# Four RMS norms of a two-block transformer kernel: sums by tokens in two columns, spread into rows by TensorE, and one weight load placed between two halves

## The reference, cut to what matters

```python
def rmsnorm(x, g):
    y = x * lax.rsqrt(jnp.mean(x * x, axis=-1, keepdims=True) + 1e-6)
    return y * g

# first block
for l in range(2):
    h = h + hybrid_mixer(rmsnorm(h, norm_mix[l]), ...)          # norm1 of layer l
    h = h + expert_choice_ffn(rmsnorm(h, norm_ffn[l]), ...)
x = rmsnorm(h, norm_final)                                      # f norm
# second block
x = x + sincos_2d(256)
sh1, sc1, gt1, sh2, sc2, gt2 = split(silu(c) @ ada_w + ada_b, 6)
hx = rms_norm(x, norm1_g) * (1 + sc1) + sh1                     # x norm
x = x + gt1 * token_mixer(hx @ w_in, ...)
x = x + gt2 * hier_moe(rms_norm(x, norm2_g) * (1 + sc2) + sh2, ...)
return rms_norm(x, final_norm_g)                                # l norm
```

## Time and profile before

| what | value |
|---|---|
| median of 3 runs | 2142.53 us (2142.21 to 2148.26) |
| profiled execution, whole | 2147.99 us |
| its span from first to last instruction | 2146.2 us |
| PE busy | 1917.2 us (89%) |
| DVE busy, ACT busy | 645.6 us (30%), 545.4 us (25%) |
| DMA | 748.52 MB, mean 349 GB/s |

### The profile page before, as it was taken

One profiled execution on the slowest core, in us unless ns is written; L12 is line 12 of the kernel. 1 busy time (PEld: TensorE's weight loads), 2 busy tenths in 40 slices (PEclk: granted clock), 3 DMA queues, 4 the chain that ended last, 5 costly groups with the idle time before them and its releaser, 6 DMA issues.

```text
span 2146.2 us, 32065 instructions
## 1 busy us (share of the span) xinstructions
PE 1917.2 (89%) x14254; PEld 1185.0 (55%) x14254; DVE 645.6 (30%) x992; ACT 545.4 (25%) x837; POOL 0.2 (0%) x4
## 2 busy tenths in 40 slices
PE   9999998787878999999898988889999998878796
PEld 8988832121312898872333433359999644444443
DVE  4476500000000548641431111057657300000001
ACT  4366300000000347530201222033544211011111
POOL 0000000000000000000000000000000000000000
PEclk9999999999999999999999999999999999999999
DMA  9734999999999962699999999974426999999996
GB/s 355 263 129 167 397 418 428 428 428 428 428 428 415 369 228 80 239 377 421 426 423 419 421 424 421 428 271 157 157 80 233 416 425 428 429 423 427 424 426 267
DMA packets 123028, 748.52 MB, mean 349 GB/s; under 512 B 6288, under 2 KB 27152, under 8 KB 83344
## 3 DMA queue, kind: packets, MB, share of 16 engines
q1 hardware_dynamic: 122896, 746.52, 85.3%
HBM read 745.45 MB, written 1.05 MB: 348 GB/s over the span
## 4 chain that ended last, share of the span: by engine, by line
PE 55%; DMA 37%; DVE 4%; ACT 2%; issue 1%; SPq 0%; DVEq 0%; ACTq 0%
PE bank L802 19%; DMA ring<-w_expert_up 12%; PE bank L893 10%; DMA ring<-w_expert_down 10%; PE bank L946 8%; DMA ring<-w_expert_gate 5%; PE bank L805 5%; DMA ring<-moe_w_up 5%; DMA ring<-moe_w_down 3%; DMA arena<-moe_w_up 2%; PE bank L924 2%; PE bank L829 1%; PE bank L1097 1%; PE bank L1118 1%; PE bank L1170 1%
## 5 line engine op out<-in xcount | busy, mean ns | idle before, releaser
L893 PE MATMUL bank<-ring,arena 128*32 128x512 f32 (+1 forms) x3232 | 518.2, 509 | 85.1 <-DMA ring<-w_expert_up 39.4
L893 PEld LDWEIGHTS bank<-ring,arena 128*32 128x32 f32 x3232 | 164.8, 109 | 407.4 <-issue 210.9
L946 PE MATMUL bank<-ring,arena 128*32 128x512 f32 x1280 | 279.3, 606 | 48.2 <-DMA ring<-w_expert_down 38.5
L802 PE MATMUL bank<-arena_parts,ring_parts 128*128 128x256 f32 x1296 | 293.9, 283 | 0.0
L802 PEld LDWEIGHTS bank<-arena_parts,ring_parts 128*128 128x128 f32 x1296 | 218.6, 189 | 6.6 <-ACT arena_parts L1722 2.3
L946 PEld LDWEIGHTS bank<-ring,arena 128*32 128x32 f32 x1280 | 68.8, 111 | 238.9 <-issue 171.0
L1722 ACT ACTIVATE arena<-bank 128x512 f32<-128x512 f32 (+1 forms) x142 | 73.7, 544 | 452.3 <-PE bank L908 216.3
L2265 DVE TENSOR_TENSOR arena<-arena,bank 128x512 f32<-128x512 f32 x24 | 15.8, 685 | 553.7 <-PE bank L893 553.7
L802 PE MATMUL bank<-extra_parts,ring_parts 128*128 128x256 f32 x512 | 144.2, 282 | 0.0
L802 PE MATMUL bank<-ring_parts 128*128 128x256 f32 x688 | 132.4, 284 | 1.8 <-DVE ring_parts L2694 0.9
L802 PEld LDWEIGHTS bank<-ring_parts 128*128 128x128 f32 x688 | 109.0, 189 | 4.0 <-DVE ring_parts L2694 1.2
(11 more groups left out here) (385 smaller groups left out, 2391.1 us busy)
## 6 DMA issues: line engine op xcount, KB each, us to landing
ring<-w_expert_down SPq DMA_DIRECT2D x62, 2048.0 KB, 24.0
ring<-w_expert_gate SPq DMA_DIRECT2D x58, 2048.0 KB, 23.4
ring<-w_expert_up SPq DMA_DIRECT2D x54, 2048.0 KB, 25.6
ring<-w_in SPq DMA_DIRECT2D x32, 2048.0 KB, 11.7
ring<-moe_w_up SPq DMA_DIRECT2D x24, 2048.0 KB, 28.3
ring<-moe_w_gate SPq DMA_DIRECT2D x20, 2048.0 KB, 37.9
arena<-moe_w_down SPq DMA_DIRECT2D x16, 2048.0 KB, 34.0
ring<-ada_w SPq DMA_DIRECT2D x12, 2048.0 KB, 16.9
```

The lines of the kernel that those rows point to most:

```text
L802: last = pe.matmul(out[:, n * S:(n + 1) * S], w[:, k, n * P:(n + 1) * P], x[:, k, :], start=first, stop=final)
L893: last = pe.matmul(to[own_rows(half, e)].rearrange("p (q c) -> p q c", c=own), x_slots[:, c, 32 * e:32 * e + 32], w[:, k, half], start=c = ...
L946: last = pe.matmul(banks[4 + e // PAIRS][own_rows(half, e), :].rearrange("p (x d) -> p x d", x=2), hidT[:, e // PAIRS * own + f % own, own ...
```

## The change

For norm1 of layer 1, f norm, x norm and l norm the squared chunk becomes the weight side of the sum: 16 products of one column each (8 chunks, two halves of 128 tokens), which leave the sums of 256 tokens as two columns of 128 partitions. Root and reciprocal work on 128x2. DVE then multiplies the identity by the two columns into two diagonal blocks, and PE multiplies a tile of ones by them, which puts the row of inverse roots on every partition of the PSUM bank; the eight products read that bank in place of SBUF. The 16 idle products behind x norm's sums become 8 behind f norm's rows and 6 behind x norm's rows. In layer 1 the load of unit 18 goes between unit 0's two halves. The 20 idle products of layer 0 are written at another place in the loop, with nothing between the old place and the new one, since `ADA_WITH[0]` has no entry for unit 0.

```diff
+        root_cols, inv_cols = rms[:, 0:TH], rms[:, TH:2 * TH]
+        inv_diag = rms_inv.rearrange("p (h t) -> p h t", h=TH)
...
+            def token_sums_part(step, sq, j, out, prior, **back):
+                pe.wait_ge(act_done, act_at(f"{prior} {j}", loops, **back))
+                for k in (2 * j, 2 * j + 1):
+                    for half in range(TH):
+                        last = pe.matmul(out[:, half:half + 1], sq[:, k, half * P:(half + 1) * P], ones[:, 0:1],
+                                         start=k == 0 and half == 0, stop=k == DC - 1, skip_group_check=True)
+                if j == 3:
+                    last.then_inc(pe_done, pe_p.mark(step + " sum"))
+
+            def inverse_rows(step, out, **back):
+                pe.wait_ge(dve_done, dve_at(step + " diag", loops, **back))
+                pe.matmul(out[:, 0:S], ones, rms_inv, start=True, stop=True).then_inc(pe_done, pe_p.mark(step + " rows"))
...
                 for j in range(4):
-                    sum_squares_part("norm1", squares, j, norm_bank, "squares")
+                    if layer:
+                        token_sums_part("norm1", squares, j, norm_bank, "squares")
+                    else:
+                        sum_squares_part("norm1", squares, j, norm_bank, "squares")
+                if layer:
+                    inverse_rows("norm1", take(6, "dve", "hn1 3"))
...
             for j in range(4):
-                sum_squares_part("f norm", hn3, j, norm_bank, "f squares")
+                token_sums_part("f norm", hn3, j, norm_bank, "f squares")
+            inverse_rows("f norm", take(6, "dve", "first block 3"))
+            idle_products(banks[4], 8)
             norm_bank = take(7, "act", "x norm root")
             for j in range(4):
-                sum_squares_part("x norm", hn3, j, norm_bank, "x squares")
-            idle_products(banks[4], 16)
+                token_sums_part("x norm", hn3, j, norm_bank, "x squares")
+            inverse_rows("x norm", take(7, "dve", "x normed 3"))
+            idle_products(banks[4], 6)
...
-            root("f norm", bank=banks[6])
+            root("f norm", TH, root_cols, banks[6])
...
+            def inverse_diag(step, **back):
+                dve.wait_ge(act_done, act_at(step + " root", loops, **back))
+                dve.reciprocal(inv_cols, root_cols).then_inc(dve_done, dve_p.mark(step + " inv"))
+                dve.wait_ge(dve_done, dve_at(step + " inv", loops, **back))
+                dve.tensor_tensor(inv_diag, ident.unsqueeze(1).broadcast_to([P, TH, P]),
+                                  inv_cols.unsqueeze(2).broadcast_to([P, TH, P]), ALU.mult)\
+                   .then_inc(dve_done, dve_p.mark(step + " diag"))
+                dve.wait_ge(pe_done, pe_at(step + " rows", loops, **back))
...
-            normed_inv("x norm")
+            inverse_diag("x norm")
...
-                    last = dve.scalar_tensor_tensor(hn3[:, c, :], h3[:, c, :], gain_x[:, c:c + 1], rms_inv, ALU.mult, ALU.mult)
+                    last = dve.scalar_tensor_tensor(hn3[:, c, :], h3[:, c, :], gain_x[:, c:c + 1], banks[7][:, 0:S], ALU.mult, ALU.mult)
...
                         sp.dma_start(both[:, :, 0:JOB], rows[:, :, 0:JOB]).then_inc(first_cols_loaded, 16)
+                        if layer:
+                            free(("head", 18))
+                            load_cols(HEAD_AT[18] % RING, io["ada_w_2"], 512 * layer * ADA_UNITS)
                         load(at, both[:, :, JOB:2 * JOB], rows[:, :, JOB:2 * JOB])
+                    elif i == 18 and layer:
+                        pass
```

More of the change, by code:

```diff
@@ L1221, in ada_unit @@
                     last.then_inc(pe_done, pe_p.mark(f"ada {n}", unit_done(u)))
-                if not layer:
-                    idle_products(banks[4], 20, ones)
                 for i in range(len(IN_JOBS)):
@@ L1229, in _ @@
                             ada_unit(n)
+                    if i == 0 and not layer:
+                        idle_products(banks[4], 20, ones)
                     if i > 1:
@@ L1709, in _ @@
             for j in range(4):
[L1710 to L1713, removed]
+                token_sums_part("l norm", hn3, j, banks[0], "tile2b squares", **{"pass": 1})
+            inverse_rows("l norm", banks[0], **{"pass": 1})
         @block.scalar
@@ L1891, in _ @@
                     squared("squares", j)
-                root("norm1", bank=banks[6])
+                if layer:
+                    root("norm1", TH, root_cols, banks[6])
+                else:
+                    root("norm1", bank=banks[6])
                 for j in range(4):
@@ L2053, in _ @@
                 chunk_squared("x squares", j)
-            root("x norm", bank=banks[7])
+            root("x norm", TH, root_cols, banks[7])
             for j in range(4):
@@ L2210, in _ @@
             act.wait_ge(pe_done, pe_at("l norm sum", loops, **one_back))
-            act.activation(rms_root, banks[0][:, 0:S], ACT.Sqrt, bias=eps, scale=1.0 / D)\
+            act.activation(root_cols, banks[0][:, 0:TH], ACT.Sqrt, bias=eps, scale=1.0 / D)\
                .then_inc(act_done, act_p.mark("l norm root"))
@@ L2422, in _ @@
                 dve.wait_ge(params_loaded, layer * 16 + 16)
-                normed_inv("norm1")
+                inv_rows = rms_inv
+                if layer:
+                    inverse_diag("norm1")
+                    inv_rows = banks[6][:, 0:S]
+                else:
+                    normed_inv("norm1")
                 def hn1_low(j):
@@ L2434, in _ @@
                                                         par[:, Q_NORM1 + c:Q_NORM1 + c + 1],
-                                                        in_order(rms_inv.unsqueeze(1)), ALU.mult, ALU.mult)
+                                                        in_order(inv_rows.unsqueeze(1)), ALU.mult, ALU.mult)
                     last.then_inc(dve_done, dve_p.mark(f"hn1 {j}"))
@@ L2695, in low2 @@
                                   ALU.subtract).then_inc(dve_done, dve_p.mark(f"low2 {i}"))
-            normed_inv("f norm")
+            inverse_diag("f norm")
             dve.wait_ge(positions_loaded, 16)
@@ L2701, in _ @@
                 for c in (2 * j, 2 * j + 1):
-                    last = dve.scalar_tensor_tensor(h3[:, c, :], h3[:, c, :], par2[:, R_FINAL1 + c:R_FINAL1 + c + 1], rms_inv,
+                    last = dve.scalar_tensor_tensor(h3[:, c, :], h3[:, c, :], par2[:, R_FINAL1 + c:R_FINAL1 + c + 1], banks[6][:, 0:S],
                                                     ALU.mult, ALU.mult)
@@ L3025, in _ @@
             one_back = {"pass": 1}
-            dve.wait_ge(act_done, act_at("l norm root", loops, **one_back))
-            dve.reciprocal(rms_inv, rms_root).then_inc(dve_done, dve_p.mark("l norm inv"))
-            dve.wait_ge(dve_done, dve_at("l norm inv", loops, **one_back))
+            inverse_diag("l norm", **one_back)
             for j in range(4):
@@ L3032, in _ @@
                     last = dve.scalar_tensor_tensor(hn3[:, c, :], h3[:, c, :], par2[:, R_FINAL2 + c:R_FINAL2 + c + 1],
-                                                    rms_inv, ALU.mult, ALU.mult)
+                                                    banks[0][:, 0:S], ALU.mult, ALU.mult)
                 last.then_inc(dve_done, dve_p.mark(f"out {j}"))
```

## The result

The changed kernel took **2154.18 us** (median of 12 runs, 2149.0 to 2157.97). The kernel before, run 12 times (the forecast's three runs are the first of them), took 2147.94 us (2142.21 to 2152.73). The ratio is **1.0031 [1.0021, 1.0041]**: 6.7 us slower (4.5 to 8.8), at the bound of 0.3%; the medians differ by 6.2. The profiled execution has a span of 2153.1 us (before: 2146.2).

The account below looks back on a forecast made before the run. PE was taken to bound the kernel (55% of the chain, loads 37%). Layer 1 +2.0, f norm +1.2, x norm +0.5 and l norm +1.0 gave +4.7 us on 2142.53, so 2147.2 us, range 2140 to 2154.

Parts of the forecast that it names:

- The base: Whole kernel: the median of 2142.53 us for the kernel before, to which the forecast loss of 4.7 us was added.
- Durations at 2.4 GHz: At the four norms: new steps at full clock give three times -0.4 us and -1.0 for x norm, together -2.2.
- Bank reads at nothing: DVE's eight products after each norm: reading a bank costs zero, with a bound of +0.05 us a product on two.
- The clock falls in all three places: Layer 1's norm, between the blocks and the end: one-column sums let PE fall to 1.2 GHz before the rows.
- Rival 1: All norms: PE stays at 2.4 GHz through the one-column sums; -2.2 us, 2140.3 us; chance 0.18.
- rival 3: Between the blocks: DVE's work hides PE's slower passes, f and x come to zero; +3 us, 2145.5; chance 0.1.
- Rival 2: All places: clock falls early and rises late, sums lose 2 us or more, unit takes 3.6; +9 us, 2151.5; chance 0.18.
- The price of the clock: At the four norms: 1.2 GHz lengthens sums, rows, modulation unit and idle products, turning -2.2 us into +4.7.
- the terms -0.2 - 1.6 + 0.5 + 0.7 + 0.6: Layer 1's norm, in us: root -0.2, reciprocal -1.6, diagonal blocks +0.5, spreading +0.7, rows at 1.2 GHz +0.6.
- The moved load at 0.2 us at most: Layer 1: unit 18 lands near 702.3 instead of 704.95 but is wanted near 704.8, worth 0.2 us at most.
- its queue at nothing: Layer 1, SP: unit 0's second half also waits for PE to leave unit 18's slot, which costs nothing.
- Idle products "worth what the clock is": Between the blocks: 16 idle products become 8 and 6, with no size of their own apart from the clock.

Follow-up runs that it names:

- run 12: Not a label: part of "run 12 times", the kernel before executed 12 times without a change, median 2147.94 us.
- e0_after: The changed kernel run again with no edit, beside the others on one chip: 2155.12 us, ratio 1.0037 to the kernel before.
- e1_wide: The changed kernel with each sum product moving all 128 columns of ones, the root reading one column of each half: 2146.29 us, ratio 0.9993 to before.
- e2_swap: The kernel before with only unit 18's load put between unit 0's two halves in layer 1: ratio 0.9993 to before.
- e6_noidle: e1_wide without the 8 and 6 idle products between the blocks: 2148.9 us, ratio 1.0006 to the kernel before.

## Where the prediction was right, and where it failed

The sign, the mechanism and the places were right; two sizes failed, the base and the price of the clock. The time, 2154.18, lies 0.2 us over the range's upper end. Of the 7.0 us between 2147.2 and 2154.2, 5.4 are the base and 1.5 the terms. The upper end had the upper of the three runs as its base, 2148.26, which is not below the twelve runs' median; there it is the 5.7 us for the loss that were too few, for a measured 6.2. That 0.2 us is within the noise, so on which side of the end the time fell is luck; the misses of base and price are not.

**The base, the first step that failed.** "The median 2142.53 + 4.7" stood on three runs, of which two were at 2142.2 and 2142.5 and one at 2148.3. Twelve runs, these three among them, have their median at 2147.94, and 31 more beside e0_after at 2147.3. The prediction itself noted that the profiled execution's 2147.99 lay 5.5 over that median, and worked out 2152.7 for another like it; from there the miss is 1.5 us. With one execution of 2148 and one of 2148.3 among four, nothing said that the lower two were the middle.

**Durations at 2.4 GHz: right.** e1_wide shows them undisturbed: sums 3.84 (3.9 taken), rows 0.67 (0.6), reciprocal 0.17, blocks 0.42; S1 -0.53 and S3 -0.46 against -0.4 a norm, S2 -1.37 against -0.4 - 1.0. (S2 of before varies too: 33.72, and 33.3 in the two kernels that leave it alone with 3.4 us at 1.2 GHz.) The hand-over from DVE to PE was 0.15 (704.86 + 0.42 to 705.43, kernel after), not 0.04. Bank reads at nothing: confirmed (3.22 and 3.23 for eight).

**The clock falls in all three places: right.** The windows at 0.50 are where they were named (the last at 2141.55, since the end stands 5.3 us later), and e1_wide shows that the columns of the sums decide it. Rival 1 (the clock holds) fell with the window 701.15 to 704.25; rival 3 (DVE's alternation hides f and x) fell with S2's +3.14. Rival 2 had the size nearly (+9 for the 8.0 of the three stretches) and part of the way: the unit took its 3.6 us and the low clock reached the first job, but the sums lost 1.3 to 1.5 us in three norms, not 2, and only x norm's lost more.

**The price of the clock, the second step that failed.** The forecast put it at 6.9 us (from -2.2 to +4.7). After less e1_wide, S1 to S3 together, is 10.3 us, and e0_after less e1_wide 9.2. Between the blocks it is 4.5 and 4.6 where 3.1 were taken, at the end 2.0 and 2.3 where 1.4 were; in layer 1 it is 3.8 and 2.3 for 2.4, so the size taken there lies between two executions of one code. The stretch of layer 1 taken apart, after less before, from the timelines (the earlier trace rows and the rows above):

- sums to root: 5.22 - 3.73 = +1.49 (1.2 forecast, of it 1.0 for the clock);
- root to first product: 2.37 - 2.36 = 0.0, as the terms -0.2 - 1.6 + 0.5 + 0.7 + 0.6 say;
- end of ACT's copy to first job: the unit is in the way for 1.65 us, before it was 0.15: +1.50 (0.8 forecast, 1.7 as its bound);
- the first job itself, whose first products run at 1.2 GHz (0.80 us for two): +0.41, a term that the prediction didn't have;
- the two pieces left: -0.06 each.

That is +3.29 for +2.0; in e0_after, where the clock fell later, it is +1.75. f norm's first product comes 1.6 later (1.2 forecast) and l norm's 1.55 (1.0), with sums of 5.31 and 5.33 us where 4.9 and 4.7 were taken. x norm has +1.55 (0.5 forecast, bounds -1.0 and 2.0). This is the term furthest off. Its step said that eight passes, 1.9 us, are left behind the last square; 3.2 us were. It left out that the eight idle products ahead also run at half rate, so that the sums start 0.9 us late, and that at half rate eight passes take longer than the next square, so that they queue. The 1.1 us that the execution after is shorter elsewhere are -0.1 ahead of S1, -1.6 between S1 and S2, where S5 is 1.6 shorter with less time at 1.2 GHz, and +0.6 between S2 and S3, which stays open.

**The moved load at 0.2 us at most, its queue at nothing:** right (e2_swap, 0.17 us). **Idle products "worth what the clock is":** right, 1.2 us in e6_noidle's trace.

## What to carry to other kernels

Where each product loads its own 128x128 weights, fewer moving columns bought no time in these runs (3.82 us for 32 passes of one column, 3.84 of 128), and the narrow form let TensorE's clock fall, which cost 9.2 and 10.3 us in three stretches against the wide form; so in such a place keep the columns, even if only one is read, and look at the granted clock. Price an edit together with what runs behind it at either clock, the first job and the idle products included. And take the base from where all executions at hand lie, the profiled one too, rather than from a median of three.

## What the runs showed of the chip that was not expected

- PE can be busy for the whole of a window and stay at 1.2 GHz: 6.82 of 6.82 us at 0.50 in x norm's one-column sums, while the same sums over 128 columns rose to 1.00 on their way (e6_noidle).
- Executions of one code differ in where the clock falls. The router's stretch in code that was the same took 18.19 us in before and 14.99 in e2_swap. Its windows in these two, before first:

```profile
937.77:955.90 18.13, 15.90 (x250) 14.02 (x249) 8.61 (x33) 7.55 (x14) 0.00 (x0) 0.81 0.87 342
```

```profile
936.00:952.00 16.00, 13.91 (x261) 12.65 (x260) 9.22 (x33) 7.56 (x14) 0.00 (x0) 1.00 0.96 382
```

0.81 and 1.00 are the granted clock: 3.2 us between two executions, where twelve runs of the kernel before spread over 10.5 us (2142.21 to 2152.73). How much of that spread comes from the clock is open.
- A float32 reciprocal of 2 columns took 0.17 us where one of 256 took 1.75, while a DVE product of 256 columns took 0.42.
